# Sample attention's compression on halves of the TensorE array, in high and low parts

## What is computed

```python
def compress(rows, pe, w1, w2):          # rows (B, L, 2, 64), L = 4096
    sub = rows.reshape(B, n_sub, 16, 2, 64)          # n_sub = 256
    u = einsum('bnsgd,jsdh->bjngh', sub, w1.reshape(2, 16, 64, 64))
    pre = einsum('sd,sdh->h', pe, w1) + u[:, 0, 0:255] + u[:, 1, 1:256]
    return einsum('bngh,hd->bngd', silu(pre), w2)
```

## Time and profile before

| | us |
|---|---|
| median of 3 runs | 1761.31 (1759.12 to 1766.47) |
| profiled execution | 1759.75 |
| its span | 1757.9 |
| PE busy | 1673.5 |
| DVE busy | 1147.0 |
| ACT busy | 781.6 |
| POOL busy | 426.6 |

### The profile page before, as it was taken

How to read it: one execution, slowest core, us unless ns; L and a number is a source line. 1 busy time by engine, 2 the same in 40 slices (tenths; PEclk the granted TensorE clock), 3 DMA queues, 4 the chain that set the end, 5 groups by cost and what they waited for, 6 DMA issues and landing times. The chain is left out here.

```text
span 1757.9 us, 32955 instructions
## 1 busy us (share of the span) xinstructions
PE 1673.5 (95%) x11975; PEld 1435.2 (82%) x11975; DVE 1147.0 (65%) x2535; ACT 781.6 (44%) x1652; POOL 426.6 (24%) x546
## 2 busy tenths in 40 slices
PE   6999999999998989988878999999999999999999
PEld 5999999788886856555546877999999999977887
DVE  6632248776676745565354368887778788687885
ACT  6322453777775535445334234322322232365342
POOL 1321111776664643343341001000000000040000
PEclk9999999999999999999998999999999999999999
DMA  6623111121001366566674231322222332593343
GB/s 164 106 98 115 47 43 26 28 50 27 18 12 37 88 250 199 168 210 230 210 258 173 73 99 64 115 91 97 90 90 94 107 113 84 175 383 96 93 120 108
DMA packets 158859, 204.25 MB, mean 116 GB/s; under 512 B 55110, under 2 KB 109423, under 8 KB 158674
## 3 DMA queue, kind: packets, MB, share of 16 engines
q1 hardware_dynamic: 136058, 121.66, 23.3%
q0 software_dynamic: 22368, 80.46, 13.2%
q10 hardware_dynamic: 312, 0.52, 0.1%
HBM read 164.69 MB, written 37.90 MB: 115 GB/s over the span
## 5 line engine op out<-in xcount | busy, mean ns | idle before, releaser
L3073 PE MATMUL banks<-u_sum,w_sum 128*128 128x264 f32 x2904 | 358.1, 284 | 2.7 <-DVE w_sum L3104 2.7
L3073 PEld LDWEIGHTS banks<-u_sum,w_sum 128*128 128x128 f32 x2904 | 355.0, 189 | 4.4 <-DVE w_sum L3104 4.3
L494 PE MATMUL banks<-u_parts_mix,w_in_parts 128*128 128x352 f32 x1440 | 248.2, 329 | 3.4 <-DVE u_parts_mix L877 3.4
L494 PEld LDWEIGHTS banks<-u_parts_mix,w_in_parts 128*128 128x128 f32 x1440 | 232.0, 189 | 8.5 <-DVE u_parts_mix L877 3.8
L2177 ACT ACTIVATE turned<-banks 128x512 f32<-128x512 f32 (+1 forms) x136 | 78.7, 587 | 144.7 <-PE banks L2040 116.7
L2052 PE MATMUL banks<-turned,cmp_w 128*128 128x512 f32 x256 | 133.8, 605 | 6.7 <-DVE turned L2179 3.7
L3412 PE MATMUL banks<-wd_hi,gd_hi 128*128 128x512 f32 x308 | 120.2, 390 | 1.4 <-DVE gd_lo L3443 1.0
L3412 PE MATMUL banks<-wd_lo,gd_hi 128*128 128x512 f32 x308 | 120.0, 390 | 0.0
L2040 PEld LDWEIGHTS banks<-consts,rows_grouped 128*128 128x128 f32 x512 | 64.4, 144 | 68.0 <-issue 59.8
L3412 PE MATMUL banks<-wd_hi,gd_lo 128*128 128x512 f32 x308 | 119.9, 389 | 0.0
L3300 POOL DMA_DIRECT2D rest_whole<-g_rest x1 | 0.6, 594 | 466.6 <-issue 466.6
(11 more groups left out here) (474 smaller groups left out, 3440.6 us busy)
## 6 DMA issues: line engine op xcount, KB each, us to landing
gd_whole<-g_sums SPq DMA_DIRECT2D x77, 256.0 KB, 2.7
g_sums<-silu_gate SPq DMA_DIRECT2D x55, 256.0 KB, 2.1
w_gate_raw<-in_w_gate SPq DMA_DIRECT2D x11, 1024.0 KB, 5.5
w_up_raw<-in_w_up SPq DMA_DIRECT2D x11, 1024.0 KB, 5.3
w<-in_w_down POOLq DMA_DIRECT2D x33, 256.0 KB, 19.2
w_in_raw<-in_w_in SPq DMA_DIRECT2D x29, 256.0 KB, 3.4
g_sums<-s SPq DMA_DIRECT2D x22, 256.0 KB, 2.3
x_tile<-in_x_prompt SPq DMA_DIRECT2D x8, 512.0 KB, 4.5
```

The source lines that it names most:

```text
L494: mm = nc.tensor.matmul(bank[:, 0:PIECE], w[:, pb, :], u[:, pa, k, tokens(p)], start=(k == 0 and (pa, pb) == TERMS[0]), stop=(k == KT - 1 ...
L3073: mm = nc.tensor.matmul(bank(tg, i), wp[side, p][:, a, k, :], m.u[tg, i, b][:, k, :], start=(k == 0 and (a, b) == TERMS[0]), stop=(k == kh ...
```

## The change

- The order by head is no longer made. A `comp` fill is turned straight from the ring, in 8 turns of 64 rows: for each of 2 tokens and 2 chunks, the rows 0 to 63 and the rows 64 to 127 are turned beside each other into two banks, (2, 3) or (4, 5).
- ScalarE copies each such fill, rounding it to fp32r (the high part), and VectorE subtracts this from PSUM (the low part), for every `comp` fill.
- The product is 12 fp32r products of 256 columns: 2 tokens x 3 terms (high x high, high x low, low x high) x 2 heads, each head with the 64 rows of its half, in banks (0, 1) or (6, 7).
- The first MLP weights are loaded in a layout that holds each head's half of the array, K in the SSD stage and V in this one, and are split into parts at the start in 8 pieces on ScalarE (`w1_hi`) and VectorE (`w1_lo`).
- `shift`, `add`, `hidden`, `project` and `take` come one fill later; `project` writes into the unit's own bank. `kc(0)` moves from inside unit 9 to behind the first four `keys(0)` fills, and with it the chain that norms the keys and chooses the blocks. SSD scalings go behind every second ScalarE copy.
- `load_values(0)` moves behind the loads of `w_out`, and the second of these waits until unit 15 is used. A compression chunk's slot is free when it was turned.

```diff
+def load_cmp_weights(sp, io, raw, kv, loaded):
+    for j in range(2):
+        for half in range(2):
+            sp.dma_start(raw[64 * half:64 * half + 64, :, j, :],
+                         io.cmp_w1[0, kv, CSTRIDE * j:CSTRIDE * (j + 1), :, :].rearrange("t d h -> d t h")).then_inc(loaded, 16)
...
-    fills += comp(9, range(6)) + kc(0) + comp(9, range(6, 8)) + comp(10) + keys(0) + win(0)
+    fills += comp(9) + comp(10) + keys(0, range(1)) + kc(0) + keys(0, range(1, 8)) + win(0)
...
+    project_at = {at["comp", u, 7] + 5: u for u in range(16)}
+    END = [at["kc", hb, 0] - 15 for hb in range(2)]
+    cmp_bank = lambda u, g: m.bank[((0, 1), (6, 7))[pair_of(u)][g]]
+    score_bank = lambda hb, j: m.bank[(6, 0)[hb] + (j + 1) % 2]
+    turn_pair = lambda f: m.psum[:, (2, 4)[cmp_number[f] % 2] * 512:][:, 0:1024].rearrange("p (a c) -> p a c", a=2)
...
-            return order[f][2] % 2 == 1 or order[f][2] == 4
+            return True
...
-                load_values(0)
...
                 for k in range(W_SPLIT_EARLY):
+                    if k == 1:
+                        used(sp, "comp", 15, 7)
                     sp.dma_start(m.w_out_first[:, k, :], io.w_out[0, k * P:(k + 1) * P, :]).then_inc(m.w_out_in[k], 16)
+                load_values(0)
...
-                            pool.wait_ge(s.grouped, 4 * hb + 2 * h + sh + 1)
+                            pool.wait_ge(s.turned, at["comp", hb, 4 * h + 3] + 1)
...
+                        for t in range(2):
+                            for h in range(2):
+                                src = ring(("comp", u, q // 4, h))[:, (2 * (q % 4) + t) * P:(2 * (q % 4) + t + 1) * P]
+                                for a in range(2):
+                                    rows = slice(64 * a, 64 * a + 64)
+                                    x = nc.tensor.transpose(turn_pair(f)[:, a, 64 * (2 * t + h):64 * (2 * t + h) + 64],
+                                                            src[rows, :], c("ident")[rows, rows])
...
-                    mm = nc.tensor.matmul(m.bank[u % 2][:, :], m.cmp.w1[:, u % 2, q, :, :].rearrange("p j h -> p (j h)"),
-                                          w.fill[:, f % SLOTS, :], start=(q == 0), stop=(q == 7))
+                    for t in range(2):
+                        for i, (weights, x) in enumerate(((w.w1_hi, hi), (w.w1_hi, lo), (w.w1_lo, hi))):
+                            for g in range(NG):
+                                rows = slice(64 * g, 64 * g + 64)
+                                mm = nc.tensor.matmul(cmp_bank(u, g)[:, 0:256], weights(u % 2, 2 * q + t)[rows, :],
+                                                      x[rows, 256 * t:256 * t + 256], start=(q == 0 and t == 0 and i == 0),
+                                                      stop=(q == 7 and t == 1 and i == 2))
...
+                def low_part(f):
+                    n = cmp_number[f]
+                    dve.wait_ge(s.copied_a, copies_before[f])
+                    if n >= LOWS:
+                        used(dve, "comp", (n - LOWS) // 8, (n - LOWS) % 8)
+                    nc.vector.tensor_tensor(by_halves(w.fill_lo[:, n % LOWS, :]), turned_halves(f),
+                                            by_halves(w.fill_hi[:, f % SLOTS, :]).bitcast(F32), ALU.subtract).then_inc(s.split, 1)
...
-                for G in range(2):
-                    for h in range(2):
-                        group(G, h)
+                w1_lo(0)
```

More of the change, by code:

```diff
@@ L1517, in _ @@
             def _(sp):
-                for kv in range(2):
-                    for j in range(2):
-                        src = io.cmp_w1[0, kv, 16 * j:16 * (j + 1), :, :].rearrange("(q s) d h -> (s d) q h", s=2)
-                        sp.dma_start(w.w1[:, kv, :, j, :], src).then_inc(s.cmp_loaded, 16)
+                load_cmp_weights(sp, io, w.raw, 0, s.cmp_loaded)
                 for b in range(0, DB, 2):
@@ L1928, in copied @@
         def copied(engine, f):
-            engine.wait_ge(s.copied_a if ACT_FILLS[f] else s.copied_v, copies_before[f])
+            if f in cmp_number:
+                engine.wait_ge(s.split, cmp_number[f] + 1)
+            else:
+                engine.wait_ge(s.copied_a if ACT_FILLS[f] else s.copied_v, copies_before[f])
         def used(engine, *fill):
@@ L2008, in turn @@
                         return
-                    if f >= 3:
-                        copied(pe, f - 3)
+                    for e in sorted({max(e for e in range(f) if bank in banks_of(e)) for bank in banks_of(f) if f >= 2}):
+                        copied(pe, e)
                     kind, hb, i = order[f][:3]
@@ L2013, in turn @@
                         u, q = hb, i
-                        G = 2 * u + q // 4
-                        pe.wait_ge(s.grouped, 2 * G + 2)
-                        pieces = [(w.xr[:, G % 2, h, g * 512 + (q % 4) * P:g * 512 + (q % 4 + 1) * P], P)
-                                  for g in range(NG) for h in range(2)]
+                        if q % 4 == 0:
+                            for h in range(2):
+                                chunk_here(pe, ("comp", u, q // 4, h))
+                        if u == 11 and q == 0:
+                            pe.wait_ge(s.imp_taken, 1)
+                        for t in range(2):
+                            for h in range(2):
+                                src = ring(("comp", u, q // 4, h))[:, (2 * (q % 4) + t) * P:(2 * (q % 4) + t + 1) * P]
[3 more added lines that the diff above has]
+                                                            src[rows, :], c("ident")[rows, rows])
+                        x.then_inc(s.turned, 1)
+                        return
                     elif kind == "keys":
@@ L2093, in score @@
                     if j < 2:
-                        pe.wait_ge(s.added, 2 * (10 + j) if hb == 0 else 32)
+                        pe.wait_ge(s.taken, (10, 16)[hb])
                     elif j < 6:
@@ L2124, in weigh @@
                     copied(pe, f)
-                    if hb and i == 0:
+                    if i == 0 and hb == 0:
+                        pe.wait_ge(s.taken, 15)
+                    elif i == 0:
                         pe.wait_ge(s.o_ready, 1)
@@ L2170, in copy @@
                 bank = m.bank[3 + f % 3]
-                dst = w.kcT[:, 512 * i:512 * (i + 1)] if kind == "kc" else w.fill[:, f % SLOTS, :]
-                parts = [(dst, bank[:, :])]
+                dst = (w.kcT[:, 512 * i:512 * (i + 1)] if kind == "kc" else w.fill_hi[:, f % SLOTS, :] if kind == "comp" else
+                       w.fill[:, f % SLOTS, :])
+                parts = [(by_halves(dst), turned_halves(f)) if kind == "comp" else (dst, bank[:, :])]
                 if kind == "weights" and i == 9:
@@ L2253, in w_out_hi, with w1_hi @@
                     nc.scalar.activation(m.w_out_first_hi[:, k, :], m.w_out_first[:, k, :], ACT.Copy).then_inc(s.w_out_hi, 1)
-                ssd_roots()
+                def w1_hi(piece):
+                    if piece == 4:
+                        act.wait_ge(s.w1_in, 16 * 4)
+                    kv, tokens = piece // 4, slice(4 * (piece % 4), 4 * (piece % 4) + 4)
+                    hi = w.hi_v[:, tokens, :, :] if kv else w.hi_k[piece // 2][:, 4 * (piece % 2):4 * (piece % 2) + 4, :, :]
+                    raw = w.raw_v if kv else m.cmp.raw
+                    nc.scalar.activation(hi, raw[:, tokens, :, :], ACT.Copy).then_inc(s.w1_hi, 1)
+                w1_hi(0)
                 for f in range(n_fills):
@@ L2261, in _ @@
                         copy(act, f)
-                        if f >= 16 and scales:
+                        if f >= 16 and f % 2 == 1 and scales:
                             ssd_scale(*scales.pop(0))
-                    if f - 2 in LAST:
-                        shift(LAST[f - 2])
+                    if f % 2 == 0 and f // 2 + 1 < 8:
+                        w1_hi(f // 2 + 1)
+                    if f == 15:
+                        ssd_roots()
                     if f - 3 in LAST:
-                        hidden(LAST[f - 3])
+                        shift(LAST[f - 3])
+                    if f - 4 in LAST:
+                        hidden(LAST[f - 4])
                     for hb in range(2):
@@ L2447, in _ @@
                         copy(dve, f)
-                    if f + 4 in first_of and first_of[f + 4] >= 2:
-                        group(first_of[f + 4], 0)
-                    if f + 3 in first_of and first_of[f + 3] >= 2:
-                        group(first_of[f + 3], 1)
-                    if f - 2 in LAST:
-                        add(LAST[f - 2])
+                    if f in cmp_number:
+                        low_part(f)
+                    if f % 2 == 0 and f // 2 + 1 < 8:
+                        w1_lo(f // 2 + 1)
+                    if f - 3 in LAST:
+                        add(LAST[f - 3])
                     if f == LAST_OF_FOURTH:
                         place_queries()
-                    if f - 6 in LAST:
```

(3 more changed lines are left out.)

108 lines of the change are left out of this document (61 added, 47 removed).

## The result

The changed kernel took 1767.95 us (median of 7 runs, 1764.75 to 1768.94), the kernel before on the same chip 1761.93 (1755.50 to 1766.47). The ratio is 1.0032, with a 95% interval of 1.0016 to 1.0048: no change that counts, and if anything slower, where 1742 us was forecast with a range of 1726 to 1758. The profiled execution took 1764.75 us with a span of 1762.9; PE is busy for 1662.2 us of it, DVE 1163.2, ACT 808.8, POOL 421.6.

What follows compares the result with a forecast made beforehand. Compression was taken to be bound by PE, not by the gathers. The terms -22.4 (16 units), -1.7 (start), +2, +2.5 and +1.5 sum to -18.1 us against 1759.75, so 1742 us, range 1726 to 1758.

Steps and rivals of the forecast that it cites:

- Products and turns: Compression fills: 12 products in overlapping pairs 0.73 us, 8 turns 0.30 us, so PE 1.03 us a fill in place of 1.29.
- The chain of ScalarE and VectorE: Compression: turns, copy and subtraction take 1.9 us for two fills against PE's 2.06; 0.4 us a unit added, 9.4 us.
- the chain decides: Rival for compression: copy and subtraction in series make a fill 1.15 to 1.2 us, a unit 10.1, total 1753; chance 0.20.
- The start: Start of sample attention: first turn needs no grouping, so the first product comes at about 629.4; 1.7 us less (0 to 2).
- The splitting of w1: Fills up to f = 14: 0.6 us on ACT and on DVE at every second fill, hidden under PE's time.
- The norm, the choice of blocks, the values: Unit 10's stall +2 us, choice of blocks in `keys(0)` +2.5, `load_values(0)` on SP's queue among chunks of values +1.5.
- TensorE waits for its own instructions: Rival for compression: gaps of 1.7 us a unit lose 27 us over 16 units, result 1758 to 1769; chance 0.08.

Runs made afterwards that it cites:

- x1: Changed kernel without VectorE's subtraction for each fill, products taking the rounded rows for the low part; ratio 0.9950 to the kernel before, units 9.4 us.
- y2: The changed kernel again, unaltered, in an execution of the second kind; ratio 1.0012 to the kernel before, units 9.4 us.
- first kind: Runs, the result's among them, in which the kernel before took 1760 to 1762 us.
- y3: Changed kernel with V's weights loaded in the SSD stage and w1's pieces split sooner, second kind; ratio 0.9938 to the kernel before.
- second kind: Runs in which the kernel before took 1738 to 1740 us.
- x4: Changed kernel with V's weights loaded in the SSD stage and 5 chunks gathered early in place of 7, first kind; ratio 1.0023 to the kernel before.
- x8: Kernel of y3 with the SSD row sums' Ln and Exp, and the scalings, moved behind `key_roots(0)`, first kind; ratio 1.0027 to the kernel before.
- z5: The kernel of x8 again, in the second kind; ratio 0.9947 to the kernel before.
- z4: The kernel of y3 again, on another chip, second kind; ratio 0.9930 to the kernel before.
- y1: The kernel before, run for its own trace on the same chip as y2 and y3, second kind; ratio 1.0000, units 10.8 us.
- x5: Changed kernel with one small whole-array product behind each fill's turns, giving the signal in their place, second kind; ratio 1.0211 to the kernel before.
- x7: Changed kernel with 4 whole-array turns a fill in place of 8 on halves, second kind; ratio 1.0208 to the kernel before.
- y4: The kernel of x5 again, on the same chip as y2, second kind; ratio 1.0231 to the kernel before.

## Why the prediction was wrong

- *Products and turns* were right. The starts of pairs are 0.12 us apart, the two of a pair 3 ns. A fill whose turns are not held up costs 1.01 us where 1.03 was worked out, and a unit 9.4 (x1, y2). That 1.01 and 1.03 are so near is in part luck: from the first turn to the first product it is 0.21 us (716.72 to 716.93 in the result's trace) for the 0.30 taken, and from there to the next turn 0.79 (716.93 to 717.72) for 0.73.
- *The chain of ScalarE and VectorE* failed as a sum for the executions of the result. The step "the turns (0.3, and 0.2 to the end of the last), the copy 0.59, the subtraction 0.69, and three hand-overs, small beside these: 1.9 us for two fills" has each duration right (0.59 and 0.69 measured). What failed in it is "small beside these": the hand-over from TensorE is 0.42 us in the mean. That makes 2.3 us for two fills, 1.15 a fill against TensorE's own 1.01; with the 1.3 us that a unit has beside its fills (9.4 - 8 x 1.01: about 0.8 for the second product and its changes, 0.4 to 0.5 of the wait at its end) a unit is 10.5 us. So the rival *the chain decides* is what happened, from a lag and not from slower passes; its 10.1 us was nearly the size. By the Trainium skill (TensorEngine Tiling, PSUM Bottleneck), whose rule stood beside that rival, emptying PSUM may become the bottleneck: the trace agrees in the first kind, where TensorE is idle for 8% of steady compression and x1 takes that away, and hardly in the second, where the chain costs the forecast's 0.4 us of a unit's 9.4. The price of the failed step over 16 units is 16 x 1.0 = 16 us.
- *The start* failed outright, and in both kinds: "V's weights are 1 MB on SP's queue, needed 8 us after the start, when rings are not yet full". The rings were full: their share was 1.10 and 1.04 from 630 to 650 us. The trace of before had shown it, 1.03 and 1.00 from 640 to 660 us without V's weights. Before, then the result:
```profile
640.00:650.00 10.00, 8.06 (x37) 4.63 (x36) 4.64 (x8) 5.13 (x9) 5.17 (x5) 1.00 1.03 403
650.00:660.00 10.00, 10.00 (x50) 6.07 (x50) 5.83 (x10) 4.59 (x11) 3.47 (x5) 1.00 1.00 385
```
```profile
630.00:640.00 10.00, 5.05 (x71) 3.84 (x70) 4.31 (x7) 3.13 (x6) 6.96 (x7) 0.96 1.10 221
640.00:650.00 10.00, 6.83 (x73) 6.11 (x72) 3.87 (x7) 4.15 (x8) 1.87 (x2) 0.67 1.04 374
```
The forecast was -1.7 us; the first second product came 9.2 us later than before in the result and 12.5 in y2. Loading the weights in the stage before gave 13.6 us back (y3) and 14 in total time, so in the second kind the late weights are the cause. In the first kind, the result's own, they are not shown to be all of it: with the weights early the first second product comes at 653.5 (x4) and 658.1 (x8) in place of 659.4, and the whole is no shorter. There the standstills without a wait take a share of the 9.2 us that no run separates. I had charged the load's bytes to a queue and never asked when the last of them would land and who stands behind it: ScalarE's in-order queue, and so every copy.
- *The splitting of w1: hidden.* By itself, yes. But moving `ssd_roots` from the empty start into fill 15 was in the diff, though not in the list of the change, and had no term in the sum; it cost 4.0 us in unit 1 (13.4 against 9.4 in z5), about 3 in the result (13.5 against 10.4).
- *The norm, the choice of blocks, the values*, forecast at +6. Unit 10, where the norm now falls, is 2.3 us over a steady unit in the result, 1.7 (y2) to 4.5 us (z4) in the second kind. But units 8 to 10 of before, with `kc(0)` and the norm in them, are together 4.8 us over three steady ones (6.5 in y1), so this stall fell where it was forecast to grow by 2. `keys(0)` took `kc(0)` in and changed by only -0.9 us (result) and +0.6 (y2 against y1, 33.4 to 34.0), so the +2.5 was too dear. The last stretch changed by 0.0 and by +2.9 us (78.9 in y2, 76.0 in y1).
- *TensorE waits for its own instructions*, priced at nothing in the forecast and 27 us in the rival, is real in the first kind, but is not in every unit: 15.0 us over sample attention, 3.8 of them from 629 to 662 us, where the kernel before has 9.4. The trace of before shows it in compression too, at 643 us, with the rings full:
```profile
643.03 1.12 PE L2052 MATMUL banks<-turned,cmp_w 128*128 128x512 f32 x2 [1.25 <-issue]
```

In sum, the profiled execution is 22.8 us over the 1742 forecast. By my estimate from the rows above these are 16 for the late signals, 10.9 for the start (9.2 later in place of 1.7 sooner), 3 for the roots and 2 for unit 15's end (6.3 us over a steady unit, 4.0 before), less 9 for the norm, the choice and the values (about -3 in place of +6).

In the second kind, y2 against y1 from one second product to another: the first comes 12.5 us later; ten units on, -13.7 (10 x -1.4, the roots' +4.0, the placing of queries +1.0, and 5 us less than before for `kc(0)`, which has left this stretch); to unit 11's +2.8; three units more -3.6; to unit 15's +1.5; to the stage's end +1.1. That is +0.6 us.

What stays open: what makes an execution one of the first kind, and whether the late signals of steady units come from the halves. For the halves speaks that the kernel before, in the same kind, has none in 45 there. Against them as the only cause speak its 25 late signals elsewhere, all on the whole array. An untested rival is the number of instructions: a fill of the changed kernel has 20 products and turns with 20 loads in 1.01 us, one of before has 6 with 6 loads in 1.3 us. x5 and x7 would have told, had they met the first kind. How much of the result's late start is V's weights stays open too.

## What to carry to other kernels

A load that an in-order queue waits for is priced by when its last byte lands on rings as full as that stage's own gathers make them, not by its bytes; put it in the stage before if there is room. (Here that gained 12 us against the kernel before in one kind of execution; in the other, x4 and x8 gained nothing.) When TensorE gets faster, write the loop through the emptied banks as one sum with each hand-over in it, and ask what the sum is if one of them is 0.4 us: a cover of 0.16 us is none. And every line that the diff moves needs its own term, table loads included.

## What the runs showed of the hardware

- Two products on the two row halves run side by side at 256 columns too: 0.12 us a pair, as one of 264 columns on the whole array.
- A change between half and whole array costs 0.1 to 0.15 us (x7); one small whole-array product in each fill (x5) costs 0.40 us a fill in the unit's time, (12.6 - 9.4) / 8.
- In some executions the semaphore of a turn in a steady stream on halves is raised 0.4 us late in the mean and up to 1.3, while that of the second product, on the whole array, is at 0.01 us in the same 80 us. Outside the steady units signals of whole-array turns are late as well, by up to 4.0 us (25 of 210 in the kernel before, none of 224 in y1).
- In the same executions TensorE can fall to one or two products or turns each 0.72 us for 4 us (x8, with the rings at a share of 0.86).
- The kernel before itself takes about 1739 us or 1760 us, on one and the same chip (in the measurements with x1 to x4 and y1 to y4). Its compression is alike in both (10.8 us a unit); 6.4 us of the difference lie in `keys(0)` with `win(0)` (39.8 and 33.4) and 15 in the last stretch (91.4 and 76.0).
